# Decoder block with a mixture of experts: where the gathered path is divided into two branches

## The reference

```
h = rms_norm(x, norm_ffn)
combine = weights of the 2 experts chosen inside the best of 4 groups, else 0     # (tokens, 32)
for e in range(32):
    hid = silu(h @ w_gate[e]) * (h @ w_up[e])       # 1024 -> 256
    y   = y + combine[..., e:e+1] * (hid @ w_down[e])   # 256 -> 1024
x = x + y
out = rms_norm(x, norm_final)
```

## Time and profile before

| | |
|---|---|
| time, median of 3 runs | 636.9 us (636.53 to 636.95) |
| the profiled execution's own time | 637.33 us |
| its span, first to last instruction | 635.5 us |
| mean granted TensorE clock | 0.982 |
| TensorE busy | 599.0 us (94% of the span) |
| VectorE / ScalarE busy | 215.6 us (34%) / 146.0 us (23%) |
| moved by DMA | 158.96 MB, mean 250 GB/s |

### The profile page before, as it was taken

One profiled execution on the slowest core, in us unless ns is written; L12 is line 12 of the kernel. 1 busy time (PEld: TensorE's weight loads), 2 busy tenths in 40 slices (PEclk: granted clock), 3 DMA queues, 4 the chain that ended last, 5 costly groups with the idle time before them and its releaser, 6 DMA issues.

```text
span 635.5 us, 11807 instructions
## 1 busy us (share of the span) xinstructions
PE 599.0 (94%) x4974; PEld 433.6 (68%) x4974; DVE 215.6 (34%) x584; ACT 146.0 (23%) x367; POOL 19.9 (3%) x23
## 2 busy tenths in 40 slices
PE   8999999999999999999999999999989887888595
PEld 7988888878777877878888888895435424434152
DVE  3153348716343766456221232334110110111022
ACT  3111234032235353443321000001201120110014
POOL 1000000000300003001000000000000000000000
PEclk9999999999999999999999999999989989899699
DMA  8584344842112111103236997988999999999994
GB/s 324 190 335 152 123 143 179 304 160 68 68 68 69 68 68 68 68 5 121 88 123 226 425 420 318 382 346 328 424 420 419 420 419 416 422 421 420 419 402 168
DMA packets 27192, 158.96 MB, mean 250 GB/s; under 512 B 2800, under 2 KB 7040, under 8 KB 9344
## 3 DMA queue, kind: packets, MB, share of 16 engines
q1 hardware_dynamic: 24128, 137.71, 55.2%
q10 hardware_dynamic: 3008, 20.45, 7.7%
HBM read 157.07 MB, written 1.07 MB: 249 GB/s over the span
## 4 chain that ended last, share of the span: by engine, by line
PE 58%; issue 22%; DMA 12%; DVE 4%; SPq 2%; ACT 1%; POOL 0%; POOLq 0%; DVEq 0%; ACTq 0%
PE bank L621 25%; PE bank L1250 6%; DMA table<-experts 4%; DMA hT<-experts 4%; PE bank L1311 4%; PE bank L848 3%; PE bank L1204 3%; PE bank L1320 3%; DMA ring<-front 3%; PE bank L957 2%; PE bank L653 2%; PE bank L986 2%; PE bank L1006 1%; SPq L576 1%; DVE work L1838 1%
## 5 line engine op out<-in xcount | busy, mean ns | idle before, releaser
L621 PE MATMUL bank<-hT,ring 128*128 128x256 f32 x864 | 199.6, 383 | 0.7 <-DMA ring<-front 0.4
L621 PEld LDWEIGHTS bank<-hT,ring 128*128 128x128 f32 x864 | 159.7, 190 | 30.9 <-issue 10.5
L621 PE MATMUL bank<-yT,ring 128*128 128x256 f32 x256 | 55.4, 379 | 0.0
L621 PEld LDWEIGHTS bank<-yT,ring 128*128 128x128 f32 x256 | 48.6, 190 | 6.6
L1838 DVE TENSOR_TENSOR work<-bank,table 128x512 f32<-128x512 f32 (+1 forms) x22 | 11.6, 544 | 95.3 <-PE bank L1204 89.6
L1204 PEld LDWEIGHTS bank<-work,tok 128*128 128x128 f32 x256 | 30.1, 192 | 12.7 <-issue 12.0
L1204 PE MATMUL bank<-work,tok 128*128 128x128 f32 x256 | 31.7, 278 | 3.5 <-issue 3.5
L1250 PE MATMUL bank<-ring,work 128*32 128x512 f32 x272 | 34.5, 596 | 0.3 <-ACT work L1452 0.2
L1452 ACT ACTIVATE work<-bank 128x512 f32<-128x512 f32 (+2 forms) x45 | 23.3, 519 | 49.1 <-PE bank L1311 37.9
L1311 PE MATMUL bank<-ring,work 128*32 128x512 f32 (+1 forms) x160 | 33.0, 672 | 1.1 <-ACT work L1452 1.1
L1320 PE MATMUL bank<-work 128*128 128x512 f32 (+1 forms) x68 | 30.1, 582 | 1.4 <-ACT work L1452 0.7
(11 more groups left out here) (262 smaller groups left out, 734.5 us busy)
## 6 DMA issues: line engine op xcount, KB each, us to landing
ring<-front SPq DMA_DIRECT2D x47, 1024.0 KB, 5.2
ring<-experts SPq DMA_DIRECT2D x42, 1024.0 KB, 23.7
work<-experts SPq DMA_DIRECT2D x9, 1024.0 KB, 27.3
ring<-experts ACTq DMA_DIRECT2D x8, 1024.0 KB, 14.9
table<-experts SPq DMA_DIRECT2D x6, 1024.0 KB, 26.5
yT<-experts SPq DMA_DIRECT2D x6, 1024.0 KB, 26.9
hT<-experts SPq DMA_DIRECT2D x4, 1024.0 KB, 23.5
work<-experts ACTq DMA_DIRECT2D x3, 1024.0 KB, 28.0
```

Of the source, the lines that this page charges most:

```text
L621: return first(pe.matmul(o, l, r, start=(k == 0), stop=(k == n - 1)))
```

## The change

One line sets which groups stand in the first and in the last block. It is read by TensorE, ScalarE and VectorE alike.

```diff
-FIRST_GANGS, LAST_GANGS = range(NGANG // 2), range(NGANG // 2, NGANG)
+FIRST_GANGS, LAST_GANGS = range(1), range(1, NGANG)
```

## The result

The changed kernel takes 638.43 us (median of 21 runs) against 637.38 us for the kernel before in the same comparison. The ratio is 1.0013 with a 95% interval of 1.0007 to 1.0019, so 0.83 us slower (0.45 to 1.2), less than the 1.3 us that I called measurable but clear of zero over this many runs. The forecast was no change; it was the rival with the starved stream that came true. One of the 21 executions took 652.98 us at a granted clock of 0.932 and is left out of the ratio.

The account below looks back on a forecast made before the run. The prediction took the expert chunk stream to bound the kernel. Nothing gained at the old place and 0 to 0.1 us lost at group 1 gave 636.9 to 637.0 us against the median of 636.9; range 636.1 to 638.5.

Parts of the forecast that it names:

- the rival with the starved stream: At group 1 the chunk stream runs dry as the clock falls behind the jump; 637.6 to 639.4 us, chance 0.32.
- What bounds the kernel: From about 445 us to the end, the expert chunk stream; a TensorE delay counts only by the time the stream is dry.
- What goes, at the old place: Between groups 3 and 4, TensorE would be 4.53 us earlier without the jump, worth nothing by itself.
- Both pieces: TensorE, groups 3 and 4: 3.45 us of jump over the dense code, and 1.08 us more in group 4's gate/up matmuls.
- What comes, ScalarE and VectorE: At group 1 their jumps fit in idle time of 7.14 and 9.41 us before their first work.
- the moved code traffic: Instruction transfer moving from 525 to 528 us into an equally full stream: about 0.1 us, moved with the jump, nil.
- What comes, TensorE: At 459.4 us, group 1 starts 3.45 us later, up to 4.53 behind its first gate/up matmuls; costs 0 to 0.1 us.
- the second piece: 1.08 us more before the fourth gate/up matmul of group 4; could be absent or larger at group 1.
- The margin: Group 1's first chunk issue, at 464.81, may come as late as 469.2 without a gap; the jump leaves 0.9 us.
- Rival B: At group 1's gather and first gate/up, half clock delays the first issue past 469.2; likeliest 637.8 us, chance 0.32.
- the prediction's C: TensorE, not the stream, sets the end, so the 1.08 us might be saved: 635.8 us, chance 0.09.
- D: The jump costs nothing at the new place, or a stall stays at the old one: 636.9 us, chance 0.07.

Follow-up runs that it names:

- 12 and 20 idle matmuls: Kernel before, with 12 or 20 useless matmuls on TensorE ahead of the gather of group 1; ratios 1.0027 and 1.0072.
- behind group 1: Kernel before with all three engines divided behind group 1 (first block groups 0 and 1) in place of group 3; ratio 0.9997.
- the second experiment: Kernel before with only ScalarE and VectorE divided behind group 0, TensorE still behind group 3; ratio 0.9997.
- TensorE alone: Kernel before with only TensorE divided behind group 0, ScalarE and VectorE still behind group 3; ratio 1.0009.
- 8 idle matmuls: Kernel before, with 8 useless matmuls on TensorE ahead of the gather of group 1; ratio 1.0005.

## Why the prediction was wrong

**What bounds the kernel**: right. The stream of chunks sets the end, and the cost of a stall is near the time that the stream stands dry (12 and 20 idle matmuls; none behind group 1). In the changed kernel it is less, 0.8 of 1.9 us, which is not explained.

**What goes, at the old place**: right. Both pieces vanished (3.54 us, L1250 7.05 us) and nothing was gained by it.

**What comes, ScalarE and VectorE**: right for the time (the second experiment). I had put the moved code traffic at nil. By the rate that is near enough (416 against 419 GB/s at the old place), but landings come 2.1 us later locally in that experiment, which I didn't foresee; the end did not move.

**What comes, TensorE: this is the step that failed.** "TensorE starts group 1 later by 3.45 us, or by up to 4.53" was mis-sized: it measured 5.54 us, 3.81 by the jump and 1.72 by the half clock. The jump was near the price of its row, and the second piece, which I had left open, was absent. Missing was the half clock. With it the first issue came behind the 469.2 that I had worked out as the latest, and the stream ran dry. I left it out because the one jump in the trace was followed by full clock; that row was one draw of something that varies, as the two profiles of TensorE alone show, and the 6.56 us at the old place itself.

**The margin**: I worked out 4.4 us (464.81 to 469.2). 3.5 us late is free within the error, 5.2 us is not; so its size held, though it is no sharp edge: at 3.5 us late the rate had begun to fall. With the right lateness it gives 5.54 - 4.4 = 1.1 us of loss against 0.83 (0.45 to 1.2) measured. That closeness is partly luck: by its rate the stream lost 1.9 us, and 12 idle matmuls, with the same hole, cost 1.7.

**Rival B** had the mechanism, the place and the deciding point right, and its likeliest figure, 0.8 us of loss, is the measured one; here too with some luck, since its issue was 5.15 us late in place of 5.54. I gave it 0.32. Four of five profiles say that it should have had more, and the rule on the free-running watch pointed that way.

**The other rivals**: the prediction's C, that TensorE sets the end, is refuted by the division behind group 1; D, that the stall stays or vanishes, by the timeline.

No version here beats the kernel before. The division behind group 1 equals it.

## What to carry to other kernels

A stall on an engine that only releases buffers costs nothing while the transfers already issued last longer than the stall; so look up, at the place where the stall would stand, when the last issued transfer lands and how late the next issue may come. Price a pause of TensorE with the half clock behind it (1.7 to 2.8 us more on the gather here) even where the one trace at hand shows none, and let the cover be judged against the sum. Judge a hole by the rate of the DMA engines: a single landing can be late without one. In this kernel a jump over unused code is a stall of 3.3 to 3.9 us in each of twelve profiles, to be put where the store is deep, neither at the thin start nor behind the last wait.

## What the runs showed that I had not expected

The second piece of the jump depends on how the code lies. With no other change than idle matmuls placed before it, the jump at the old place is followed by a second "issue" of 0.96 us (8 idle matmuls), 3.52 us (12) and 5.44 us (20), where before had 1.08 us in all. The chain of the kernels with 12 and with 8:

```profile
528.15 3.44 issue
531.59 2.15 PE bank L1204 x17
533.74 3.52 issue
537.26 3.08 PE bank L1204 x15
```

```profile
526.46 3.56 issue
530.02 4.56 PE bank L1204 x25
534.58 0.96 issue
535.54 0.94 PE bank L1204 x7
```

TensorE stops after 25, 17 and 1 of the 32 matmul records of the gather, 8 and then 16 earlier for the 8 and then 16 idle records more. So the stop stands at a fixed place of the program. And it goes on 9.1, 9.1 and 9.2 us after the first piece began, before 534.54 - 525.77 = 8.8: at nearly a fixed time. I read this as a second block of code that is under way; the piece is what TensorE reaches it too early by. In the profile with the half clock of 6.56 us at the old place there is no second piece.

That is the second piece for which the prediction named the Trainium skill (Runtime: NRT & Kernel Launch, section "Instruction fetch mechanics": code comes in blocks, and a taken branch out of the blocks held has to fetch its target). The trace agrees in kind. The times of 8.8 to 9.2 us are this case's. The Trainium skill's rule that the clock's activity watch runs free of the program (TensorE: Matmul & The Clock Gate, section "What's actually happening") agrees too: 3.83 us and 5.45 us for the same gather in two executions of one program.
